# One instruction instead of two for the high and low parts of two neighbouring weight units

## The chip, the cores and the metric

The kernel runs on one core of a Trainium2 chip. The metric is the device time of one execution in microseconds (us); lower is better. Engines are named as in the profile: PE is TensorE (PEld its weight loads), DVE is VectorE, ACT is ScalarE, POOL is GpSimd, SP is SyncE, which here issues the weight transfers.

## The reference

Two transformer blocks run one after the other on 256 tokens of width 2048, in float32, and every dense product reads its weights once from HBM. Cut to its products:

```
# first block
h = rmsnorm(x);  qkv = h @ w_qkv                      # 2048 x 6144
y = [diff_attention, stick_breaking_attention, chunk_band_attention]
x = x + y @ w_o
h = rmsnorm(x)
g = causal_dwconv(h @ w_gate);  u = h @ w_up          # 2048 x 5632 each
x = x + (silu(g) * u) @ w_down
x = rmsnorm(x)
# second block
h @ w_in;  mla_mixer;  dsa_mixer (top-k keys);  x = x + [a, b] @ w_out
x = x + memory_cross_attention(rmsnorm(x), rmsnorm(mem))
x = x + square(relu(rmsnorm(x) @ w_up)) @ w_down      # d_ff = 8192
out = rmsnorm(x)
```

## The kernel before

**Units.** All weights are cut into 804 units. A unit is 128 rows by 1024 columns of float32 (512 KB; the eight units of the stage `tail` have 800 columns, the four of `k_nope` 512). Units form groups, one per pair of PSUM banks (`group_banks`): a "turned" group (`qk`, `gate`, `up1`, `up2` and others) has 4 units and writes a transposed result, a "straight" group (`v`, the `o`, `out` and `down` stages) has 2 to 8. All groups with more than one unit start at an even unit and end at an odd one.

**A unit's way.** PE multiplies in float32 with split operands: `w = hi + lo`. For each unit
- SP issues the transfer into one of 4 slots of `raw_w` (line 1705), once DVE has finished with the unit four before (semaphore `w_lo`, line 1704);
- ACT writes `hi_w` by a copy with rounding (`split_hi`, line 771). It first waits for the transfer, and for PE to have used the unit four before, whose slot it overwrites (`w_used`, line 770; PE raises it twice per unit, once per half);
- DVE writes `lo_w = raw_w - hi_w` (`split_lo`, line 1177) after `w_hi`;
- PE waits for `w_lo` (line 416) and does 16 matmuls (turned, lines 428 and 430) or 12 (straight, lines 437 to 439).

**Order.** There is no scheduler: each engine's program is written out by hand and is executed strictly in that order. `units(n)` stands in the programs of PE, ACT and DVE at corresponding places. On PE it runs the next n units. On ACT and DVE, for each unit u of them, it first splits unit u + 3 and then, if u is the last of its group, does the group's work: `turned_group` or `straight_group`. The split of u + 3 needs PE to be through with unit u - 1. Between the calls of `units` stand the attention steps, norms (`token_scales`, `pieces`, `root`), rotations and so on.

**Group work named below.** For `gate`, ACT and DVE alternate: ACT copies one half out of PSUM (L794), DVE adds the other (L1191), ACT scales for the convolution (L800), DVE adds two taps (L1196, L1199), all this for both halves; then ACT's tanh (L804) and DVE's product (L1204). `up1` and `up2` are shorter (L794, L1191, L1210 or L1215, then ACT L810 or L816 and DVE L1183). `down1_2` adds into the residual (L1235, L1238) and ACT takes sums of squares (L779), from which the next norm is made. In a step of the band attention PE does scores (L566), values (L612), a transposition (L596) and one unit; DVE does `soft` (L1433 to L1438) and `total` (L1457, on which the transposition of the same head waits), and then its share of `units(1)`.

## Time and profile before

| | |
|---|---|
| device time, median of 3 runs | 2481.21 us (2480.41 to 2484.02) |
| profiled execution: its time, its span | 2483.1 us, 2481.3 us |
| PE busy | 2417.3 us, 97% |
| DVE busy, ACT busy | 1500.9 us (60%), 1261.0 us (51%) |
| chain that ended last: PE, DVE, ACT | 94%, 2%, 2% of the span |
| mean granted TensorE clock | 0.992 of full speed |
| weight transfers | 424.7 MB, the 16 DMA engines 54.7% busy |

The span is what the profiler saw between the first and the last instruction. Because matmuls overlap, a busy PE is not PE at its peak; but idle time of PE in the waits is time in which nothing ran on it. An engine's row in the timeline gives start, duration, engine, line, operation and tiles, and in brackets how long the engine had been idle and who released it.

### The profile page before, as it was taken

To read this page: it belongs to the slowest core of one execution; us is meant where nothing else is said; L and a number is where in the kernel's file an instruction comes from. 1 tells how busy PE (TensorE), PEld (TensorE's weight loads), DVE (VectorE), ACT (ScalarE), POOL (GpSimd) and SP (SyncE) were. 2 spreads that over 40 slices of the span, in tenths; PEclk is the share of its full clock that TensorE was granted. 3 is DMA by queue.
4 is the path that set the end of the run, shared out by engine and by line. 5 is a ranking of instruction groups with operands and counts; after the bars stand their busy time and mean duration, and the time that the engine had idled before them with its cause. 6 is when DMAs were issued, how large, how long until landed. Compare 5 with 4: busy or idle time off the path is not lost.

```text
span 2481.3 us, 31755 instructions
## 1 busy us (share of the span) xinstructions
PE 2417.3 (97%) x12304; PEld 2020.1 (81%) x12304; DVE 1500.9 (60%) x2311; ACT 1261.0 (51%) x1974; POOL 5.2 (0%) x12
## 2 busy tenths in 40 slices
PE   6999999999999999999999999999999999999998
PEld 5888887788888888888877877787788888888886
DVE  5586777666666556645667544564666556556454
ACT  5466566655555435534556445555544444344343
POOL 0000000000000000000000000000000000000000
PEclk9999999999999999999999999999999999999999
DMA  6544444455555665565454544554566666666664
GB/s 211 174 162 158 136 154 147 150 188 177 197 180 191 189 189 187 192 205 185 155 180 144 178 128 134 173 169 136 160 179 193 189 187 184 194 185 191 206 187 141
DMA packets 118341, 432.11 MB, mean 174 GB/s; under 512 B 13184, under 2 KB 13328, under 8 KB 117680
## 3 DMA queue, kind: packets, MB, share of 16 engines
q1 hardware_dynamic: 117216, 424.70, 54.7%
q0 software_dynamic: 976, 5.39, 0.6%
q8 instruction: 98, 1.61, 0.3%
q14 instruction: 51, 0.42, 0.1%
HBM read 427.93 MB, written 2.11 MB: 173 GB/s over the span
## 4 chain that ended last, share of the span: by engine, by line
PE 94%; DVE 2%; ACT 2%; issue 1%; DMA 1%; ACTq 0%; SPq 0%; DVEq 0%
PE bank L428 29%; PE bank L437 15%; PE bank L439 15%; PE bank L438 15%; PE bank L430 15%; PE bank L612 1%; PE bank L454 1%; DVE lo_w L1177 1%; ACT hi_w L771 0%; PE bank L596 0%; PE bank L485 0%; DVE xT L1300 0%; PE bank L566 0%; PE bank L575 0%; PE bank L523 0%
## 5 line engine op out<-in xcount | busy, mean ns | idle before, releaser
L1177 DVE TENSOR_TENSOR lo_w<-raw_w,hi_w 128x1024 fp32r<-128x1024 f32 x804 | 968.1, 1219 | 689.8 <-ACT hi_w L771 689.0
L771 ACT ACTIVATE hi_w<-raw_w 128x1024 fp32r<-128x1024 f32 x804 | 834.0, 1053 | 678.7 <-PE bank L439 429.7
L428 PE MATMUL bank<-xT,hi_w 128*128 128x512 f32 x3008 | 1062.6, 398 | 2.9 <-DVE lo_w L1177 1.8
L430 PE MATMUL bank<-xT,lo_w 128*128 128x256 f32 x3008 | 843.6, 280 | 0.0
L428 PEld LDWEIGHTS bank<-xT,hi_w 128*128 128x128 f32 x3008 | 566.3, 188 | 139.0 <-issue 2.1
L430 PEld LDWEIGHTS bank<-xT,lo_w 128*128 128x128 f32 x3008 | 569.3, 189 | 0.2
L439 PE MATMUL bank<-hi_w,act_lo 128*128 128x512 f32 x864 | 341.2, 395 | 0.0
L438 PE MATMUL bank<-lo_w,act_hi 128*128 128x512 f32 x864 | 341.2, 395 | 0.0
L437 PE MATMUL bank<-hi_w,act_hi 128*128 128x512 f32 x864 | 341.2, 395 | 0.0
L437 PE MATMUL bank<-hi_w,xT 128*128 128x512 f32 (+1 forms) x736 | 295.0, 401 | 4.2 <-DVE xT L1300 3.4
L439 PE MATMUL bank<-hi_w,xT 128*128 128x512 f32 (+1 forms) x736 | 287.6, 391 | 0.0
L438 PE MATMUL bank<-lo_w,xT 128*128 128x512 f32 (+1 forms) x736 | 287.1, 390 | 0.0
L439 PEld LDWEIGHTS bank<-hi_w,act_lo 128*128 128x128 f32 x864 | 162.1, 188 | 39.5
L437 PEld LDWEIGHTS bank<-hi_w,act_hi 128*128 128x128 f32 x864 | 162.1, 188 | 39.4
L438 PEld LDWEIGHTS bank<-lo_w,act_hi 128*128 128x128 f32 x864 | 162.1, 188 | 39.4
L437 PEld LDWEIGHTS bank<-hi_w,xT 128*128 128x128 f32 x736 | 139.8, 190 | 32.1 <-issue 4.7
L439 PEld LDWEIGHTS bank<-hi_w,xT 128*128 128x128 f32 x736 | 139.3, 189 | 29.0
L438 PEld LDWEIGHTS bank<-lo_w,xT 128*128 128x128 f32 x736 | 139.7, 190 | 25.6
L1183 DVE TENSOR_TENSOR act_lo<-steps,act_hi 128x512 fp32r<-128x512 f32 x54 | 37.4, 692 | 39.3 <-ACT act_hi L816 23.3
L1300 DVE SCALAR_TENSOR_TENSOR xT<-bank,gains,xT 128x256 fp32r<-128x256 f32 x96 | 39.7, 476 | 20.8 <-ACT xT L872 20.6
L1230 DVE TENSOR_TENSOR x<-bank,x 128x512 f32<-128x512 f32 x80 | 51.2, 682 | 0.0
L794 ACT ACTIVATE product<-bank 128x256 f32<-128x256 f32 x88 | 33.4, 380 | 35.0 <-PE bank L430 35.0
(299 smaller groups left out, 1486.6 us busy)
## 6 DMA issues: line engine op xcount, KB each, us to landing
raw_w<-in_w_up SPq DMA_DIRECT2D x216, 512.0 KB, 4.2
raw_w<-in_w_down SPq DMA_DIRECT2D x216, 512.0 KB, 4.2
raw_w<-in_w_gate SPq DMA_DIRECT2D x88, 512.0 KB, 3.6
raw_w<-in_w_in SPq DMA_DIRECT2D x72, 512.0 KB, 3.8
raw_w<-in_w_qk SPq DMA_DIRECT2D x64, 512.0 KB, 3.6
raw_w<-in_w_v SPq DMA_DIRECT2D x32, 512.0 KB, 3.7
raw_w<-in_w_o SPq DMA_DIRECT2D x32, 512.0 KB, 3.6
raw_w<-in_w_out SPq DMA_DIRECT2D x32, 512.0 KB, 3.6
```

The lines of the kernel that those rows point to most:

```text
L428: e.matmul(pair[c][:, :], w_hi[:, cols_k], both[:, kt].rearrange("p h t -> p (h t)"), start=(kt == 0), stop=False, skip_group_check=True)
L430: last = e.matmul(pair[c][:, 0:TOK], w_lo[:, cols_k], both[:, kt, 0, :], start=False, stop=(kt == g.kts - 1), skip_group_check=True)
L437: e.matmul(out, in_hi[:, at, rows], w_hi[:, cols_k], start=(kt == 0), stop=False)
L438: e.matmul(out, in_hi[:, at, rows], w_lo[:, cols_k], start=False, stop=False)
L439: last = e.matmul(out, in_lo[:, at, rows], w_hi[:, cols_k], start=False, stop=(kt == g.kts - 1))
L454: last = e.transpose(bank[:, k * TOK + t * P:k * TOK + (t + 1) * P], src[:, t, kt * P:(kt + 1) * P], const("ident"))
L771: e.activation(hi_w[:, u % SPLIT_SLOTS, 0:unit_cols[u]], raw_w[:, u % RAW_SLOTS, 0:unit_cols[u]], ACT.Copy).then_inc(s["w_hi"], 1)
L794: e.activation(out, group_banks(n)[c][:, TOK:2 * TOK], ACT.Copy, scale=scale).then_inc(s["part_out"], 1)
L1177: e.tensor_tensor(lo, raw_w[:, u % RAW_SLOTS, 0:unit_cols[u]], hi.bitcast(F32), ALU.subtract).then_inc(s["w_lo"], 1)
L1183: e.tensor_tensor(lo, prod[:, pair % 2], hi.bitcast(F32), ALU.subtract).then_inc(s[f"act_lo{tag}_done"], 1)
L1230: e.tensor_tensor(here, bank[:, :], here, ALU.add).then_inc(s["x_added"], 1)
L1300: e.scalar_tensor_tensor(dst[:, dst0 + kt, 1, :], banks[4 + p % 4][:, k * TOK:(k + 1) * TOK], scale, dst[:, dst0 + kt, 0, :].bitcast(F32), ...
```

## The change

For two neighbouring units, an even one and the odd one behind it, ACT now writes both high parts with one instruction over the two slots (2048 columns), and DVE both low parts with one. `split_hi` and `split_lo` do nothing for an odd unit. `w_hi` and `w_lo` count pairs. Before it splits the pair (u, u + 1), ACT waits for both transfers, and for PE to have used both units whose slots are overwritten (`u - SPLIT_SLOTS + 2`). SP, which still issues one transfer per unit, waits for the pair in whose slots it loads. PE waits for `w_lo` only at even units. The slots stay four for each of the three buffers.

```diff
@@ tensor_program, units
-                    e.wait_ge(s["w_lo"], u + 1)
+                    if u % 2 == 0:
+                        e.wait_ge(s["w_lo"], u // 2 + 1)
@@ scalar_program
             def split_hi(u):
-                if u < n_units:
-                    e.wait_ge(s[f"raw_landed{u % RAW_SLOTS}"], 16 * (u // RAW_SLOTS + 1))
+                if u % 2 == 0 and u < n_units:
+                    a, cols = u % SPLIT_SLOTS, unit_cols[u]
+                    for n in (u, u + 1):
+                        e.wait_ge(s[f"raw_landed{n % RAW_SLOTS}"], 16 * (n // RAW_SLOTS + 1))
                     if u >= SPLIT_SLOTS:
-                        e.wait_ge(s["w_used"], 2 * (u - SPLIT_SLOTS + 1))
-                    e.activation(hi_w[:, u % SPLIT_SLOTS, 0:unit_cols[u]], raw_w[:, u % RAW_SLOTS, 0:unit_cols[u]],
-                                 ACT.Copy).then_inc(s["w_hi"], 1)
+                        e.wait_ge(s["w_used"], 2 * (u - SPLIT_SLOTS + 2))
+                    e.activation(hi_w[:, a:a + 2, 0:cols], raw_w[:, a:a + 2, 0:cols], ACT.Copy).then_inc(s["w_hi"], 1)
@@ vector_program
             def split_lo(u):
-                if u < n_units:
-                    hi, lo = (w[:, u % SPLIT_SLOTS, 0:unit_cols[u]] for w in (hi_w, lo_w))
-                    e.wait_ge(s["w_hi"], u + 1)
-                    e.tensor_tensor(lo, raw_w[:, u % RAW_SLOTS, 0:unit_cols[u]], hi.bitcast(F32),
+                if u % 2 == 0 and u < n_units:
+                    a, cols = u % SPLIT_SLOTS, unit_cols[u]
+                    hi, lo = (w[:, a:a + 2, 0:cols] for w in (hi_w, lo_w))
+                    e.wait_ge(s["w_hi"], u // 2 + 1)
+                    e.tensor_tensor(lo, raw_w[:, a:a + 2, 0:cols], hi.bitcast(F32),
                                     ALU.subtract).then_inc(s["w_lo"], 1)
@@ sync_program
-                    e.wait_ge(s["w_lo"], u - RAW_SLOTS + 1)
+                    e.wait_ge(s["w_lo"], (u - RAW_SLOTS) // 2 + 1)
```

ACT's order before, in the stages `gate` and `up1` (one `up1` group, then one `gate` group; `product` and `steps` are buffers of the group work, `hi_w` the split):

```order
L771 ACTIVATE hi_w<-raw_w 128x1024 [waits w_used,raw_landed2]
L794 ACTIVATE product<-bank 128x256 [waits conv_taps,w_used] x2
L810 ACTIVATE act_hi<-steps 128x512 [waits prod1]
L771 ACTIVATE hi_w<-raw_w 128x1024 [waits w_used,raw_landed3]
L771 ACTIVATE hi_w<-raw_w 128x1024 [waits w_used,raw_landed0]
L771 ACTIVATE hi_w<-raw_w 128x1024 [waits w_used,raw_landed1]
L771 ACTIVATE hi_w<-raw_w 128x1024 [waits w_used,raw_landed2]
L794 ACTIVATE product<-bank 128x256 [waits prod1,w_used]
L800 ACTIVATE steps<-product,gains 128x256 [waits sum_out]
L794 ACTIVATE product<-bank 128x256 [waits prod1,w_used]
L800 ACTIVATE steps<-product,gains 128x256 [waits sum_out]
L804 ACTIVATE steps<-steps 128x512 [waits conv_taps]
```

The same place after the change (lines are moved by three):

```order
L775 ACTIVATE hi_w<-raw_w 128x2048 [waits w_used,raw_landed3,raw_landed2]
L797 ACTIVATE product<-bank 128x256 [waits conv_taps,w_used] x2
L813 ACTIVATE act_hi<-steps 128x512 [waits prod1]
L775 ACTIVATE hi_w<-raw_w 128x2048 [waits w_used,raw_landed1,raw_landed0]
L775 ACTIVATE hi_w<-raw_w 128x2048 [waits w_used,raw_landed3,raw_landed2]
L797 ACTIVATE product<-bank 128x256 [waits prod1,w_used]
L803 ACTIVATE steps<-product,gains 128x256 [waits sum_out]
L797 ACTIVATE product<-bank 128x256 [waits prod1,w_used]
L803 ACTIVATE steps<-product,gains 128x256 [waits sum_out]
L807 ACTIVATE steps<-steps 128x512 [waits conv_taps]
```

Four splits between two groups' work have become two of double width; the one that stands right ahead of a group's work is now a pair, and waits for the last unit of that group instead of the last but one.

DVE's order before at the same place:

```order
L1204 SCALAR_TENSOR_TENSOR steps<-steps 128x512 [waits gate_tanh]
L1177 TENSOR_TENSOR lo_w<-raw_w,hi_w 128x1024 [waits w_hi] x4
L1191 SCALAR_TENSOR_TENSOR product<-bank,product 128x256 [waits part_out] x2
L1210 SCALAR_TENSOR_TENSOR steps<-steps,product 128x512 [waits sum_out,gate_silu]
L1183 TENSOR_TENSOR act_lo<-steps,act_hi 128x512 [waits act_hi1_done]
```

And after:

```order
L1209 SCALAR_TENSOR_TENSOR steps<-steps 128x512 [waits gate_tanh]
L1182 TENSOR_TENSOR lo_w<-raw_w,hi_w 128x2048 [waits w_hi] x2
L1196 SCALAR_TENSOR_TENSOR product<-bank,product 128x256 [waits part_out] x2
L1215 SCALAR_TENSOR_TENSOR steps<-steps,product 128x512 [waits sum_out,gate_silu]
L1188 TENSOR_TENSOR act_lo<-steps,act_hi 128x512 [waits act_hi1_done]
```

DVE keeps its order in the same way: nothing but the splits is merged, and the second of the two pairs stands right ahead of the group's first addition.

## Rows read from the trace of the kernel before

**Rows 1.** Page, part 1: busy us, share of the span, instructions.

```profile
PE 2417.3 (97%) x12304; PEld 2020.1 (81%) x12304; DVE 1500.9 (60%) x2311; ACT 1261.0 (51%) x1974; POOL 5.2 (0%) x12
```

**Rows 2.** Waits of PE: total us, times, longest us.

```profile
PE bank L454 <- ACT y L862: 14.3, 1, 14.3
PE bank L454 <- DVE h_nat L1290: 7.9, 2, 3.9
...
PE bank L428 <- DVE lo_w L1177: 1.8, 1, 1.8
```

**Rows 3.** Groups by form: busy us, mean ns, idle before with releaser.

```profile
L1177 DVE TENSOR_TENSOR lo_w<-raw_w,hi_w 128x1024 fp32r<-128x1024 f32 x792 | 957.4, 1224 | 683.6 <-ACT hi_w L771 682.9
...
L771 ACT ACTIVATE hi_w<-raw_w 128x1024 fp32r<-128x1024 f32 x792 | 824.5, 1056 | 671.6 <-PE bank L439 422.6 <-PE bank L430 246.3 <-DMA raw_w<-in_w_out 2.4
...
L1183 DVE TENSOR_TENSOR act_lo<-steps,act_hi 128x512 fp32r<-128x512 f32 x54 | 37.4, 692 | 39.3 <-ACT act_hi L816 23.3 <-ACT act_hi L810 16.0
...
L804 ACT ACTIVATE steps<-steps 128x512 f32<-128x512 f32 x22 | 13.9, 633 | 22.5 <-DVE steps L1199 22.5
```

**Rows 4.** Timeline of ACT at a gate group's end.

```profile
788.63 1.06 ACT L771 ACTIVATE hi_w<-raw_w 128x1024 fp32r<-128x1024 f32 x1 [1.51 <-PE bank L430]
791.46 1.06 ACT L771 ACTIVATE hi_w<-raw_w 128x1024 fp32r<-128x1024 f32 x1 [1.77 <-PE bank L430]
...
797.83 0.63 ACT L804 ACTIVATE steps<-steps 128x512 f32<-128x512 f32 x1 [1.07 <-DVE steps L1199]
798.37 2.94 ACT L771 ACTIVATE hi_w<-raw_w 128x1024 fp32r<-128x1024 f32 x3
```

**Rows 5.** Timeline of DVE there.

```profile
793.70 0.42 DVE L1191 SCALAR_TENSOR_TENSOR product<-bank,product 128x256 f32<-128x256 f32 x1
...
799.45 3.50 DVE L1177 TENSOR_TENSOR lo_w<-raw_w,hi_w 128x1024 fp32r<-128x1024 f32 x3 [0.26 <-ACT hi_w L771]
```

**Rows 6.** Timeline of ACT in two straight stages, v and down1_2.

```profile
82.12 1.06 ACT L771 ACTIVATE hi_w<-raw_w 128x1024 fp32r<-128x1024 f32 x1 [1.66 <-PE bank L439]
84.84 1.06 ACT L771 ACTIVATE hi_w<-raw_w 128x1024 fp32r<-128x1024 f32 x1 [1.66 <-PE bank L439]
...
1182.53 1.06 ACT L771 ACTIVATE hi_w<-raw_w 128x1024 fp32r<-128x1024 f32 x1 [1.74 <-PE bank L439]
1185.33 1.06 ACT L771 ACTIVATE hi_w<-raw_w 128x1024 fp32r<-128x1024 f32 x1 [1.74 <-PE bank L439]
```

**Rows 7.** Timeline of PE: after a wait for lo_w, and at the mix norm.

```profile
19.40 0.50 PE L428 MATMUL bank<-xT,hi_w 128*128 128x512 f32 x1 [1.82 <-DVE lo_w L1177]
...
1213.08 3.22 PE L454 MATMUL bank<-consts,mixed 128*128 128x128 f32 x14 [5.44 <-DVE mixed L1290]
```

**Rows 8.** Timeline of DVE at the last down1_2 group.

```profile
1206.74 0.68 DVE L1235 TENSOR_TENSOR h_nat<-bank,x 128x512 f32<-128x512 f32 x1
```

**Rows 9.** Windows: PE busy, PEld, DVE, ACT, POOL, then PEclk, DMA share, GB/s.

```profile
21.00:22.00 1.00, 1.00 (x5) 0.86 (x4) 1.00 (x4) 1.00 (x4) 0.00 (x0) 0.50 0.91 348
1609.00:1610.00 1.00, 0.00 (x0) 0.00 (x0) 1.00 (x2) 0.55 (x1) 0.00 (x0) 1.00 0.00 0
1612.00:1613.00 1.00, 1.00 (x3) 0.79 (x3) 1.00 (x2) 1.00 (x2) 0.00 (x0) 0.50 0.78 123
```

**Rows 10.** Timelines of the band attention, PE then DVE.

```profile
382.78 0.39 PE L596 MATMUL bank<-consts,a_p 128*128 128x128 f32 x2
...
382.83 0.42 DVE L1433 CUSTOM_DVE_ANT_0 a_s<-bank,rel 128x256 f32<-128x256 f32 x1
383.69 0.48 DVE L1438 SCALAR_TENSOR_TENSOR a_s<-a_s,a_small,a_p 128x256 f32<-128x256 f32 x1
384.48 0.29 DVE L1457 CUSTOM_DVE_ANT_0 a_p<-a_p,a_s 128x128 f32<-128x128 f32 x1 [0.31 <-ACT a_s L908]
```

**Rows 11.** Page, part 6: issues, KB each, median us to landing.

```profile
raw_w<-in_w_up SPq DMA_DIRECT2D x216, 512.0 KB, 4.2
mem<-in_mem POOLq DMA_DIRECT2D x1, 2048.0 KB, 9.1
```

## Prediction

> **What bounds the kernel.** I read the page's busy times first: PE 97%, DVE 60%, ACT 51% [rows 1]. Then the waits of PE: the reader is to see that what PE waits for are norms (L454 with L862 and L1290), and that in 804 units it waited for a low part once, 1.8 us at the start [rows 2]. The splits cost PE nothing. The groups by form say why: before the 792 wide splits on ACT the engine had been idle 671.6 us in all, and what ended that was PE giving a slot free; DVE was idle 683.6 us, ended by ACT [rows 3]. So the splits run as early as the slots allow, and the question is how early that still is after the change. For this I read the timelines around one gate group.
>
> **PE's pace.** ACT's splits start when PE has finished a unit, so their distance is PE's time per unit: 788.63 to 791.46, 2.83 us turned [rows 4]; 2.72 and 2.80 us straight [rows 6].
>
> **What the change removes.** Neither engine limits, so only latency counts, but the instructions first. A high part takes 1.056 us for 1024 columns, and 512 columns 0.633: 0.83 ns a column, so 2048 take 1.056 + 0.85 = 1.91 us. A low part takes 1.224 and 0.692 us: 2.29 us for 2048 [rows 3]. Single splits back to back have a distance of 0.94 us on ACT ((2.94 - 1.06) / 2) and 1.14 on DVE ((3.50 - 1.22) / 2) [rows 4, 5], so that two take 2.00 and 2.36. A pair saves 0.09 and 0.07 us; over 402 pairs 36 and 28 us of engines which are idle 40 and 49%. I cost it at nothing for PE.
>
> **What it adds: the lead.** Call T the time at which PE ends an odd unit u. Before, at that time units u+1 and u+2 were ready, and u+3, whose slot was free since T - 2.83, mostly too; a split had 3 units of PE's time minus its own 2.3 us, some 6 us to spare. Now ACT may begin the pair (u+3, u+4) only at T, and it ends at T + 0.07 + 1.91 = T+1.98. DVE runs T+2.02 to T+4.31. PE has (u+1, u+2) to do, to T+5.66 (turned), T+5.44 or T+5.6 (straight). Spare: 1.3, 1.1, 1.3 us. Where ACT and DVE have nothing else to do, that is enough, in `up2` and `down` too: `up2` has ACT at work until about T+6.5 (L816), which puts the next low part at about T+10.8, and PE wants it at T+11.3. But what stands in ACT's queue ahead of a pair now counts after 1.1 to 1.3 us instead of 6.
>
> **Term 1, gate, 22 groups.** Before, from DVE's first addition (793.70) to the end of tanh (797.83 + 0.63 = 798.46) the group's work takes 4.76 us, ACT and DVE handing each other every step [rows 4, 5]. That chain starts behind the low part that stands ahead of it; now this is a pair that ends at T+4.31. So: addition T+4.23 (instructions overlap by 0.08), tanh ends T+8.99, and only then does ACT reach the pair (u+5, u+6), whose slots were free at T+5.66: high part T+8.90 to T+10.81, low part to T+13.14. PE is through with (u+3, u+4) at T+11.3 and waits 1.85 us. To refill PE takes about 0.3 more: neighbouring units otherwise overlap by some 0.2 us (an estimate), and the first matmul after such a wait took 0.50 us [rows 7] instead of 0.40. 2.14 us. The following up1 group's chain is through by about T+18.6, before the next pair may start (T+18.9), so nothing adds up and nothing is caught up: PE was never ahead of anything. 22 x 2.14 = **47 us**.
>
> **Term 2, the clock after such waits.** The trace of before shows what an idle PE does to the granted clock. After the 1.82 us wait before 19.40 the clock was 0.50, that is 1.2 instead of 2.4 GHz, in the window 21 to 22; while PE stood still at 1609 to 1610 it was 1.00, and at 1612 to 1613, with PE busy again, 0.50 [rows 7, 9]. Windows around these show about 3.2 us at the lower level each time, beginning after PE was back: 1.6 us lost. Gate's waits are close to the shortest of these. Bounds: 0 to 22 x 1.6 = 35 us. I take six in ten, **21 us**.
>
> **Term 3, norms.** At the ends of `o_late`, `down1_2` and `ox` nothing hides the chain to the next norm. Before, the last DVE addition group began at 1206.74 and PE's transpositions at 1213.08, 6.34 us later [rows 7, 8]; PE had ended its unit at about 1207.6, so T is about 1208. Now DVE must first do the pair, whose slots are free only at T: the addition starts at T+4.2 (T+3.3 for the 800-column units) and not at T-1.3. About 4.4 us each, **13 us**. In the bursts behind `o_late` and `ox` the last quarter of the transposed input stands behind a pair again: PE finishes transposing and one unit at T+3.7, DVE's part is done at T+5.9; 2 x 2.5 = **5 us**.
>
> **Term 4, band attention.** In an odd step DVE ends the pair at T+4.31; then soft of the next head (wide, 382.83 to 384.17, 1.2 us without its wait) and total (0.29) end at about T+5.7. PE's transposition, which needs total, would be due at T+4.75 (steps of 3.9 us; it stood 0.9 us behind the unit's end, at 382.78 [rows 10]). 0.95 us, in 8 steps; in the three of these where an `o_early` group ends, DVE's two additions (1.28 us) stand between. **12 us**.
>
> **Term 5, the other places.** About 30 pairs in other attention steps (diff, stick-breaking, dsa, the index scores, the start of cross), in the rotation of the index key, in the squares of `down1_2` and in the prologue have a chain through ACT and DVE behind them that PE waits on within about one unit. Bounds: 0 each where other waits cover it, and DVE's whole 2.3 us. I take band's value, the nearest, rounded up for the groups that end there: 30 x 1.1 = **33 us** (0 to 69).
>
> The sum is 47 + 21 + 13 + 5 + 12 + 33 = 131 us on the profiled execution's own 2483.1 us (span 2481.3), which is 1.9 us above the median of 2481.21: **2612 us** against the median.
>
> The Trainium skill ("Perfetto Trace Analysis", Optimizing Scalar/DVE Operations) says both things on this change: grouping into larger operations helps where the engine is saturated, and where ACT and DVE are not saturated but cause bubbles on other engines, breaking instructions up may let work finish sooner. The trace puts this kernel in the second case (60 and 51% busy). By the first sentence alone the result would be no slower; by the second it is slower, as summed.
>
> **Rivals.**
> - *The lead is enough.* 4.31 us is less than 5.44, and the group work might slip in elsewhere. For: in `up2` and `down`, half of the units, the arithmetic says so. Against: gate's chain is read from rows and is longer than the spare. Then nothing changes: 2481 us.
> - *Faster.* PE's 64 us of idle time (2481.3 - 2417.3) end mostly with an ACT or DVE chain. If in the dense attention steps it is the number of instructions that sets the pace, the 0.16 us saved per pair lie on the path: at most some 70 attention pairs x 0.16 = 11 us, 2470 us. The point from which this decides is PE waiting in these steps before; it waited next to nothing there [rows 2].
> - *Only gate and norms.* The attention steps absorb the rest, and the clock holds: 2481 + 47 + 13 = 2541 us.
> - *The clock falls every time and attention is at its bound*: 35 instead of 21, 69 instead of 33, some 10 more for the clock after the longer waits: 2481 + 131 + 14 + 36 + 10 = 2672 us.
> - *Transfers.* Two are now issued at once, when a pair's low part is done, and must have landed 6.6 to 7 us later. One takes 4.2 us [rows 11]. If two take twice that, 8.4, a pair needs 8.4 + 4.3 = 12.7 us per two periods of 10.9 to 11.3: over 200 x 1.6, 2800 us and more. Against: 2048 KB took 9.1 us [rows 11], so that a further 512 KB costs (9.1 - 4.2) / 3 = 1.6 us and a pair some 5.8.
> - *Not done as said*: that the wide form is slower than its columns. ACT and DVE rows at 512 and 1024 lie on a line; each 0.3 us more on a pair takes 22 x 0.3 = 7 us.
>
> The Trainium skill ("VectorE: DVE Perf Modes", the TRN2 errata) has one large tile pay a fixed cost once and many small ones each time, and gives (N + 151) / 0.96 ns for a float32 tensor_tensor. This trace agrees: 1224 ns for 1024; for 2048 the formula gives 2.29 us, an estimate of that page. As a reason to merge it is worth the 0.07 us above, off PE's path.
>
> **Numbers.** Slower as summed, with its own range 2560 to 2665: 0.68. Only gate and norms: 0.14. All at their bounds: 0.07. Transfers: 0.03. The lead is enough: 0.05. Faster: 0.03. A measurement of this kernel tells 0.2%, 5 us, from no change. Slower by more than that 0.92, within it 0.05, faster 0.03. The range 2535 to 2668 leaves out the transfers, the last two and half of the tails.
>
> **What will show it.** Right: PE's waits on DVE's low part appear some 22 times with about 1.8 us each in the gate and up1 stage, in which a pair of groups takes about 2.1 to 3.7 us longer, and none in `up2` and `down`; the splits' mean is 1.9 and 2.3 us; PE busy time is nearly unchanged except for the lower clock; norm waits have grown by 4 us. Wrong: waits for lo_w also in `up2` or `down` (my 1.3 us is no spare), transfers that release ACT's splits, or no waits at gate. The weakest part is term 5.

## The result, and the profile after

| | before | after |
|---|---|---|
| median (lowest to highest), 4 runs each | 2481.49 us (2480.41 to 2484.02) | 2675.73 us (2673.27 to 2677.62) |
| ratio, 95% interval | | 1.0782 (1.0769 to 1.0796) |
| span of the profiled execution | 2481.3 us | 2673.6 us |
| PE busy; PE idle (span less busy) | 2417.3; 64.0 us | 2472.7; 200.9 us |
| mean granted TensorE clock | 0.992 | 0.968 |

The change makes the kernel 194 us slower. The forecast was 2612 us with a range up to 2668: the direction was right, the size was 64 us short, and the result lies 8 us beyond the range.

The page's busy times of the changed kernel answer to [rows 1]:

```profile
PE 2472.7 (92%) x12304; PEld 2052.9 (77%) x12304; DVE 1443.5 (54%) x1909; ACT 1183.0 (44%) x1572; POOL 5.2 (0%) x12
```

ACT and DVE work less than before, 78 and 57 us less in all. PE has the same 12304 matmuls, is busy 55.4 us longer with them, and idle 137 us longer. These two sum to the 192 us of the spans. Its waits (total us, times, longest us) answer to [rows 2]:

```profile
PE bank L429 <- DVE lo_w L1182: 44.1, 22, 3.5
PE bank L455 <- DVE h_nat L1295: 18.7, 2, 9.4
PE bank L455 <- ACT y L865: 14.3, 1, 14.3
PE bank L597 <- DVE a_small L1462: 12.2, 8, 2.7
PE bank L455 <- DVE mixed L1295: 9.8, 1, 9.8
PE bank L438 <- DVE xT L1305: 8.6, 3, 3.8
...
PE bank L438 <- DVE lo_w L1182: 6.5, 5, 1.9
```

Before, there were two waits for a low part, 1.8 us at the start and another one of 0.7 us at 1247.11, which the prediction overlooked. Now there are 27. 22 of them stand behind the gates: 1.3 to 2.3 us each, 44.1 us together. (The first row has 22 waits and 44.1 us as well, but only by chance: it holds 20 of the gates' waits, 3.5 us at the start of the program and one of 0.3; the other two gates are in the last row, with three waits of 0.9 us in `down1_2`.) Beside them stands a long list of waits for other things, nearly all of them ended by ACT or DVE. The norms' waits have grown from 7.9 to 18.7 and from 5.4 to 9.8 (the second is the mix norm of [rows 7]). The first y wait, 14.3 us, is what it was.

The groups by form (busy us, mean ns, idle before with its releasers) answer to [rows 3]:

```profile
L1182 DVE TENSOR_TENSOR lo_w<-raw_w,hi_w 128x2048 fp32r<-128x2048 f32 x396 | 907.2, 2292 | 996.8 <-ACT hi_w L775 996.0
...
L775 ACT ACTIVATE hi_w<-raw_w 128x2048 fp32r<-128x2048 f32 x396 | 757.2, 1912 | 929.6 <-PE bank L440 554.3 <-PE bank L431 363.2 <-DMA raw_w<-in_w_up 4.6
```

The wide forms cost what their columns predict, 1.91 and 2.29 us. ACT's idle time before them is ended by PE giving slots free. A transfer ended 4.6 us of it by this row, which names the three largest releasers, and 12.1 of 945.5 us by ACT's complete list of waits.

**One gate group.** The timelines of ACT, DVE and PE of the changed kernel there answer to [rows 4, 5], with T at 869:

```profile
869.02 1.92 ACT L775 ACTIVATE hi_w<-raw_w 128x2048 fp32r<-128x2048 f32 x1 [3.63 <-PE bank L431]
...
877.31 0.64 ACT L807 ACTIVATE steps<-steps 128x512 f32<-128x512 f32 x1 [1.07 <-DVE steps L1204]
877.85 1.90 ACT L775 ACTIVATE hi_w<-raw_w 128x2048 fp32r<-128x2048 f32 x1
```

```profile
870.97 2.29 DVE L1182 TENSOR_TENSOR lo_w<-raw_w,hi_w 128x2048 fp32r<-128x2048 f32 x1 [3.25 <-ACT hi_w L775]
873.18 0.42 DVE L1196 SCALAR_TENSOR_TENSOR product<-bank,product 128x256 f32<-128x256 f32 x1
...
879.78 4.57 DVE L1182 TENSOR_TENSOR lo_w<-raw_w,hi_w 128x2048 fp32r<-128x2048 f32 x2 [1.11 <-ACT hi_w L775]
```

```profile
882.13 0.50 PE L429 MATMUL bank<-xT,hi_w 128*128 128x512 f32 x1 [2.13 <-DVE lo_w L1182]
```

The gate's chain begins at T+4.2 and ends at T+9.0, ACT reaches the next pair only then (877.85, with nothing idle before it), DVE ends its low part at T+13.1, and PE has stood for 2.1 us. This is the working of the first term to within 0.1 us, except for the wait itself (2.0 on average against 1.85).

**The clock.** Windows of 1 us around the next gate's wait of 1.93 us, which ended at 906.93 (PE busy, PEld, DVE, ACT, POOL, then the granted clock, DMA share, GB/s), answer to [rows 9]:

```profile
906.00:907.00 1.00, 0.07 (x1) 0.07 (x1) 0.88 (x1) 1.00 (x2) 0.00 (x0) 1.00 0.00 0
907.00:908.00 1.00, 1.00 (x6) 0.87 (x7) 0.94 (x1) 0.58 (x3) 0.00 (x0) 1.00 0.36 33
...
909.00:910.00 1.00, 1.00 (x5) 0.90 (x4) 1.00 (x3) 0.00 (x0) 0.00 (x0) 0.50 0.94 377
910.00:911.00 1.00, 1.00 (x5) 0.81 (x4) 0.71 (x2) 0.15 (x1) 0.00 (x0) 0.50 1.04 422
...
912.00:913.00 1.00, 1.00 (x7) 0.88 (x6) 0.20 (x1) 0.00 (x0) 0.00 (x0) 1.00 1.00 352
```

PE comes back at the full clock, and from 909 to 911 has 0.50, 1.2 instead of 2.4 GHz. With the windows to the left and right of these two, 1.7 us of the full clock are lost. The same followed 11 of the 22 gates' waits, by windows of 1 us over the whole stage.

**Where it stands still in attention.** The timelines of ACT, DVE and PE of the changed kernel in the band attention answer to [rows 10], with T at 404.3:

```profile
404.34 1.91 ACT L775 ACTIVATE hi_w<-raw_w 128x2048 fp32r<-128x2048 f32 x1 [1.76 <-PE bank L440]
```

```profile
403.08 0.16 DVE L1465 RECIPROCAL a_small<-a_small 128x1 f32<-128x1 f32 x1
406.28 2.29 DVE L1182 TENSOR_TENSOR lo_w<-raw_w,hi_w 128x2048 fp32r<-128x2048 f32 x1 [3.04 <-ACT hi_w L775]
408.49 0.42 DVE L1438 CUSTOM_DVE_ANT_0 a_s<-bank,rel 128x256 f32<-128x256 f32 x1
```

```profile
404.15 0.70 PE L567 MATMUL bank<-qkT 64*128 64x256 f32 x2
410.09 0.33 PE L597 MATMUL bank<-consts,a_p 128*128 128x128 f32 x1 [0.89 <-DVE a_small L1462]
```

DVE is done at 403.24, and the next head's softmax (L1438) stands behind the pair's low part in its program. The pair waits for ACT, ACT waits for PE to end the pair's *second* unit, and so DVE stands 3.04 us before it works 2.29 us on the pair. The softmax's scores are there at 404.85, and it runs at 408.49, 3.6 us later; before, the scores were there at 382.58 (`L566`) and the softmax ran at 382.83 [rows 10]. So the merged pair, with its wait, is a piece of queue that the attention's own instructions stand behind. Term 4 of the prediction has this case, with the transposition (L597) at T+5.7; it came at T+5.8. How much ACT stands there before the ffn burst, by its waits: first before, then after.

```profile
ACT hi_w L771 <- PE bank L439: 27.0, 22, 2.8
ACT hi_w L771 <- PE bank L430: 26.4, 21, 2.4
```

```profile
ACT hi_w L775 <- PE bank L431: 85.3, 26, 5.8
ACT hi_w L775 <- PE bank L440: 81.0, 28, 10.8
```

53.4 us in 43 waits have become 166.3 us in 54.

### The profile page after: what moved, and what is told of

Same layout as the page of the kernel before. It is cut to its first block, busy times and chain, and to the rows that moved or that the text cites. A ratio compares the mean times of both kernels' runs of the same rounds, so it can differ in the third digit from the quotient of the medians.

```text
span 2673.6 us, 30498 instructions
## 1 busy us (share of the span) xinstructions
PE 2472.7 (92%) x12304; PEld 2052.9 (77%) x12304; DVE 1443.5 (54%) x1909; ACT 1183.0 (44%) x1572; POOL 5.2 (0%) x12
## 4 chain that ended last, share of the span: by engine, by line
PE 73%; DVE 12%; ACT 9%; issue 5%; DMA 1%; ACTq 0%; DVEq 0%; POOL 0%; SPq 0%
PE bank L429 21%; PE bank L438 13%; PE bank L440 13%; PE bank L439 13%; PE bank L431 10%; ACT hi_w L775 6%; DVE lo_w L1182 6%; ACT steps L803 1%; PE bank L455 1%; DVE steps L1201 1%; DVE steps L1204 1%; PE bank L613 1%; DVE x L1235 1%; DVE product L1196 1%; DVE xT L1305 0%
## 5 line engine op out<-in xcount | busy, mean ns | idle before, releaser
L1182 DVE TENSOR_TENSOR lo_w<-raw_w,hi_w 128x2048 fp32r<-128x2048 f32 (+1 forms) x402 | 917.0, 2282 | 1013.3 <-ACT hi_w L775 1012.5
L775 ACT ACTIVATE hi_w<-raw_w 128x2048 fp32r<-128x2048 f32 (+1 forms) x402 | 765.5, 1904 | 945.5 <-PE bank L440 567.7
L429 PE MATMUL bank<-xT,hi_w 128*128 128x512 f32 x3008 | 1082.4, 404 | 49.2 <-DVE lo_w L1182 44.1
L429 PEld LDWEIGHTS bank<-xT,hi_w 128*128 128x128 f32 x3008 | 576.7, 192 | 193.6 <-DVE lo_w L1182 51.1
L431 PEld LDWEIGHTS bank<-xT,lo_w 128*128 128x128 f32 x3008 | 579.2, 193 | 0.2
L438 PE MATMUL bank<-hi_w,xT 128*128 128x512 f32 (+1 forms) x736 | 301.5, 410 | 9.9 <-DVE xT L1305 8.6
L440 PE MATMUL bank<-hi_w,xT 128*128 128x512 f32 (+1 forms) x736 | 292.3, 397 | 0.0
L438 PEld LDWEIGHTS bank<-hi_w,xT 128*128 128x128 f32 x736 | 143.7, 195 | 40.7 <-issue 9.2
L440 PEld LDWEIGHTS bank<-hi_w,xT 128*128 128x128 f32 x736 | 142.1, 193 | 30.3
L819 ACT ACTIVATE act_hi<-steps 128x512 fp32r<-128x512 f32 x32 | 20.2, 632 | 103.7 <-DVE steps L1220 103.7
L803 ACT ACTIVATE steps<-product,gains 128x256 f32<-128x256 f32 x44 | 26.5, 602 | 78.4 <-DVE product L1196 78.4
```

Of the source, the lines that this page charges most:

```text
L429: e.matmul(pair[c][:, :], w_hi[:, cols_k], both[:, kt].rearrange("p h t -> p (h t)"), start=(kt == 0), stop=False, skip_group_check=True)
L431: last = e.matmul(pair[c][:, 0:TOK], w_lo[:, cols_k], both[:, kt, 0, :], start=False, stop=(kt == g.kts - 1), skip_group_check=True)
L438: e.matmul(out, in_hi[:, at, rows], w_hi[:, cols_k], start=(kt == 0), stop=False)
L440: last = e.matmul(out, in_lo[:, at, rows], w_hi[:, cols_k], start=False, stop=(kt == g.kts - 1))
L775: e.activation(hi_w[:, a:a + 2, 0:cols], raw_w[:, a:a + 2, 0:cols], ACT.Copy).then_inc(s["w_hi"], 1)
L803: e.activation(conv1[:, pair % 2, c], out, ACT.Identity, bias=gain("convb", tile), scale=gain("conv2", tile)).then_inc(s["conv_base"], 1)
```

## The experiments

Unless said otherwise, they start from the changed kernel, written so that the form of a pair is chosen by its number p, on each engine: `wide` is the change's form; `one` is two instructions, each at its own place with its own wait, as before; `twin` is two instructions of 1024 columns at the pair's place. `w_hi` and `w_lo` count units again, and a wide instruction adds 2, which changes no wait.

All results in one table. The columns behind the ratio are stage lengths of each profile: up to the ffn burst; ffn burst, gate, up1, down1 ("ffn"); mix norm to dsa and out ("mix"); memory and cross attention ("mem"); ox; mlp burst, up2, down2, end ("mlp"). They end where PE's transpositions of the next norm begin.

| kernel | us | ratio to before (95%) | start | ffn | mix | mem | ox | mlp |
|---|---|---|---|---|---|---|---|---|
| before | 2481.5 | 1 | 460.6 | 752.5 | 397.0 | 108.1 | 28.3 | 734.8 |
| after | 2675.7 | 1.0782 (1.0769-1.0796) | 515.0 | 830.8 | 431.7 | 125.7 | 35.0 | 735.4 |
| 1 single, pair's waits | 2710.7 | 1.0922 (1.0905-1.0938) | 524.6 | 845.2 | 434.9 | 126.3 | 38.0 | 742.4 |
| 2 wide in ffn only | 2567.1 | 1.0346 (1.0331-1.0362) | 465.7 | 834.5 | 397.4 | 108.1 | 28.3 | 734.9 |
| 3 wide from unit 548 | 2491.7 | 1.0042 (1.0027-1.0058) | 461.1 | 753.3 | 396.1 | 106.6 | 33.7 | 737.0 |
| 4 single at 22 pairs | 2625.9 | 1.0586 (1.0568-1.0603) | 515.5 | 775.4 | 432.2 | 126.6 | 35.3 | 735.6 |
| 5 third slot pair in ffn | 2619.9 | 1.0562 (1.0539-1.0585) | 516.3 | 769.7 | 434.2 | 126.9 | 35.2 | 737.3 |
| 6 wide on ACT only | 2613.6 | 1.0532 (1.0512-1.0553) | 484.6 | 819.4 | 422.5 | 119.5 | 31.9 | 734.8 |
| 7 wide on DVE only | 2601.6 | 1.0483 (1.0465-1.0502) | 489.6 | 794.7 | 418.2 | 123.4 | 36.2 | 735.5 |
| 8 waits filled | 2675.4 | 1.0781 (1.0759-1.0804) | 515.3 | 820.5 | 435.6 | 125.9 | 35.2 | 740.5 |
| 9 only the place | 2516.1 | 1.0145 (1.0127-1.0162) | 476.3 | 749.4 | 407.6 | 115.9 | 31.1 | 730.6 |
| 10 one step later | 2605.2 | 1.0500 (1.0485-1.0514) | 475.2 | 832.6 | 415.1 | 106.9 | 34.5 | 739.0 |
| 11 wide from unit 560 | 2484.7 | 1.0014 (1.0005-1.0023) | 460.8 | 752.4 | 396.9 | 108.1 | 28.3 | 736.4 |
| 12 before, third slot pair | 2482.4 | 1.0007 (0.9997-1.0016) | 459.3 | 753.2 | 396.3 | 106.6 | 29.9 | 733.1 |
| 13 = 5 and 10 | 2538.3 | 1.0228 (1.0214-1.0242) | 476.6 | 766.2 | 416.5 | 106.5 | 34.4 | 736.5 |
| 14 before, one step later | 2491.1 | 1.0037 (1.0025-1.0050) | 464.5 | 752.2 | 404.5 | 106.5 | 29.0 | 733.7 |
| 15 = 2 with filled waits | 2551.6 | 1.0279 (1.0265-1.0293) | 465.6 | 815.7 | 397.0 | 108.1 | 28.3 | 734.9 |

### 1. Single instructions with the pair's waits

```
 def hi_form(p), lo_form(p):
-    return 'wide'
+    return 'twin'    # waits of the pair, then two instructions of 1024 columns
```

> The split of a pair is again two instructions of 1024 columns on each engine, as before the change, but with the waits of the changed kernel: both units' weights landed and both units' slots used before the first of them starts, VectorE starts when both high parts are there, and TensorE when both low parts are. If the lost lead is the cause (a slot pair is given back only when its second unit is used), the time is that of the changed kernel or a little over it, since a pair takes 2 x 1.06 + 2 x 1.22 = 4.6 us in place of 4.3: 2670 to 2720 us, and TensorE waits for low parts again. If the wide instruction itself is the cause (its form, or what two engines do at the same time over 2048 columns), the time goes back to 2481 to 2500 us.

2710.7 us. The loss is all there, and 35 us more, without a single wide instruction. So it is the waits, and not the form: that the wide form is slower than its columns, or disturbs something, is out. The wide form by itself is the better one, as its 0.16 us a pair says.

### 2 and 3. Wide in one stretch of the program

```
-    return 'wide'
+    return 'wide' if 128 <= p < 392 else 'one'     # 2
+    return 'wide' if p >= 548 else 'one'           # 3
```

> Wide pairs only in the units of gate, up1 and down1 (128 to 391); everywhere else one instruction for each unit, as before. If the stages' differences between the two traces are each the stage's own, this gives 2481 + 78 = 2559 us (2550 to 2570). If only the 22 waits after the gates count (the prediction's first term), 2481 + 44 to 47 = 2525 to 2530 us. If the slower clock is one effect of the whole program rather than of each wait, the time lies elsewhere, above 2570.

> Wide pairs only in up2 and down2 (units 548 to 803, a third of all), one instruction for each unit elsewhere. Lost lead: these stages have a spare of 1.1 to 1.3 us left and show no wait, so 2481 to 2484 us, no change. Were the wide form or the paired transfers the cause, a third of the loss of 194 us would show: 2530 to 2545 us.

2567.1 and 2491.7 us. In 2 the ffn stage has the changed kernel's length (834.5 against 830.8) and every other stage after it the old one: the loss is local to each stage. 3 was expected at no change and came out 9 us slower than the kernel before in the same session (2482.3). The table has 5.4 of them in ox, before the mlp norm. PE's timeline of kernel 3 there:

```profile
1750.84 1.51 PE L466 MATMUL bank<-consts,h_nat 128*128 128x128 f32 x6 [9.40 <-DVE h_nat L1314]
```

9.40 us in place of 3.9: the pairs around this burst do what the third term says of a norm. That I had put the start of the wide stretch in front of the norm was my oversight; number 11 moves it.

### 4. Single instructions at 22 pairs

```
+    return 'one' if p % 8 == 0 and (136 <= p <= 256 or 296 <= p <= 336) else 'wide'
```

These are the pairs behind a gate's chain.

> The changed kernel, with the 22 pairs whose split stands behind a gate's chain on both engines (the third pair after each gate group) split by one instruction for each unit. If the chain that holds back the pair's low part is the wait of 1.9 to 2.1 us after each gate, these waits go to 0 to 0.5 us: 2676 - 22 x 2 = 2632 us if the clock stays as low in this stage, and 2676 - 60 to 78 = 2598 to 2616 us if the low clock there comes from these waits. If another thing (transfers, the form) makes them: 2665 to 2680 us.

2625.9 us, 50 less with 22 of 402 pairs changed, and between the two times that I had given for a clock that stays low and one that recovers. What is left of the waits for low parts at the pairs made single (L1201; ten waits, nine of them 0.3 to 0.4 us and one 0.95):

```profile
PE bank L440 <- DVE lo_w L1201: 3.4, 9, 1.0
...
PE bank L449 <- DVE lo_w L1201: 0.3, 1, 0.3
```

The stage is 55.4 us shorter. PE's busy time in it went from 771.4 to 754.9, 16.5 us less, and its idle time by 38.9. By windows of 1 us the clock no longer falls behind a gate, so I put the 16.5 us down to it. The gates' part of the loss is measured by this.

### 5. A third pair of slots

```
+RINGS = ((140, 352),)      # in these units hi_w and lo_w have 6 slots; the two more lie in h_nat1's memory
-                        e.wait_ge(s["w_used"], 2 * (u - SPLIT_SLOTS + 2))
+                        e.wait_ge(s["w_used"], 2 * (before_of[u] + 2))   # the unit before in the same slot
```

The two programs split a pair two units earlier there; `raw_w` keeps four slots, and the loads come in pairs.

> The changed kernel with wide pairs everywhere, and in units 140 to 351 a third pair of slots for the high and low parts (memory that is free there), so that a pair's split starts one pair of units earlier (5.4 us). Lost lead: the 20 waits behind the gates in that stretch go to 0 and with them the low clock: 2676 - 20 x (2.0 + 0.75) = 2621 us (2612 to 2632), although every instruction of the split is as wide as before. If the wide form makes the waits: 2665 to 2680 us. If the loads are late, since the raw weights still have four slots, TensorE waits for low parts at other places and it lies between.

2619.9 us. Every split is as wide as in the changed kernel, the loads come in pairs as there, and 21 of the 22 waits behind the gates are gone; the one left, 2.3 us at 551, lies ahead of the third slot pair. With number 1 this closes the square for these waits: single instructions with the pair's lead have them, wide ones with more lead don't. It also rules out the wide form and the pairing of the loads as their cause. The stage is still 17 us longer than before: that first gate, one new wait of 2.4 us in its burst, three in `down1_2` (3.5), 4.4 more at the mix norm, and 4 us of PE's busy time. The Trainium skill ("Perfetto Trace Analysis", Optimization Strategy) says that the same gap repeating on the engine which should be saturated can mean that memory for the next tile is short, buffer count included. Here that holds: 22 gaps of about 2 us, and one more pair of slots removed 21 of them.

### 6 and 7. Wide on one engine only

```
 hi_form: 'wide'   lo_form: 'one'     # 6
 hi_form: 'twin'   lo_form: 'wide'    # 7, each of ACT's two with the wait for its own slot
```

> ScalarE makes the high parts of a pair with one instruction (it starts when both slots are free, T, where T is the end of the pair's second unit on TensorE); VectorE makes the low parts one unit at a time, the second one a step later in its program. Lost lead: the first low part is there at T + 1.98 + 1.22 = T + 3.2, so 2.3 us are left where the changed kernel has 1.1 to 1.3; after a gate the chain holds the second low part until about T + 9.2 and TensorE wants it at T + 8.2, a wait of 1 us, 22 times. Time about 2481 + 22 + some 40 in the other stages: 2540 us (2515 to 2590). If the loss is all VectorE's wide instruction: 2481 to 2490; if all ScalarE's: 2665 to 2680.

> The reverse: ScalarE makes the two high parts with two instructions that stand behind each other in its program, each with the wait for its own slot alone, so that the first runs before T and the second at T; VectorE makes both low parts with one instruction at T + 1.1 to T + 3.4. Lost lead: spare 2.1 us in place of 1.1 to 1.3; behind a gate's chain both high parts (2.1 us) and the low parts (2.3) still stand behind each other and the pair is there at T + 12.6 where it is wanted at T + 11.3, a wait of 1.3 us, 22 times. Time about 2481 + 29 + some 60 in the other stages: 2570 us (2530 to 2620). If the loss is all ScalarE's wide instruction: 2481 to 2490; if all VectorE's: 2665 to 2680.

2613.6 and 2601.6 us, the first 24 us above the range that I gave, the second inside its range. Each engine's half costs over 60% of the whole, so the halves don't add: either is enough to tie the second unit's end to the first one's split. In 6 I had put 1 us on each gate. PE there waits for low parts of turned units 45.7 us in 29 waits, 1.4 to 2.1 us at a gate; the second unit's low part stands in DVE's program behind the whole gate chain.

### 8 and 15. The waits filled with matmuls

```
+                    if u % 8 == 0 and (136 <= u <= 248 or 296 <= u <= 328):
+                        ...            # wait for the bank, as the group's first matmul does
+                        for _ in range(4):
+                            e.matmul(pair[0][:, :], xT[:, 0, 0, 0:P], xT[:, 0].rearrange("p h t -> p (h t)"),
+                                     start=True, stop=False, skip_group_check=True)
```

> The changed kernel, and at 20 of the 22 waits behind a gate TensorE does four extra matmuls of 512 columns (their result is overwritten, 4 x 0.4 = 1.6 us) ahead of the wait for the low part, so that it stands idle 0.4 to 0.5 us there in place of 2.0. Nothing else changes, and the low part comes at the same time. If the lower clock after a wait is brought on by the idle time of that wait, it stays at 1.00 there and the time falls by 20 x 0.75 = 15 us (0.75 us a wait is what the run with the 22 pairs split singly showed in TensorE's busy time): 2655 to 2665 us. If the clock has another cause: 2674 to 2680 us. If the extra matmuls run into the wait's end, more than 2680.

2675.4 us: no change. PE's timeline of kernel 8 at one gate, then windows of its clock behind the next gate, and behind the one after that, which has no filling:

```profile
872.57 1.11 PE L429 MATMUL bank<-xT 128*128 128x512 f32 x4
...
874.81 0.50 PE L446 MATMUL bank<-xT,hi_w 128*128 128x512 f32 x1 [1.12 <-DVE lo_w L1203]
```

```profile
901.00:902.00 1.00, 1.00 (x8) 0.86 (x7) 1.00 (x1) 0.00 (x0) 0.00 (x0) 1.00 0.75 225
...
926.00:927.00 1.00, 1.00 (x4) 0.78 (x3) 1.00 (x2) 0.00 (x0) 0.00 (x0) 0.50 0.83 299
```

The four matmuls overlap and take 1.1 us, not 1.6, so 1.1 us of idle time is left; they end before the low part comes, as meant. The clock stays at 1.00 behind all 20 filled waits; of the two without filling (2.1 and 2.3 us, ended at 924.69 and 1164.67) the first is followed by 0.50. The distance from gate to gate, which in the changed kernel alternated between some 24.7 and 26.3 us (waits that end at 855.95, 882.13, 906.93 and 933.25), is 24.7 to 25.3 now. The stage is 10.3 us shorter, but in this profile mix and mlp are 3.9 and 5.1 longer. Why is not known: in `up2` the matmuls of 512 columns take 399 ns on average against 394 in the changed kernel, at a granted clock of 1.00 in both, but the kernel before has 399 there too, in an mlp stage of 734.8 us. To separate this, number 15 does the same in kernel 2, where the rest of the program is as before:

> Wide pairs in units 128 to 391 alone, with TensorE's four extra matmuls ahead of 20 of the 22 waits; without them this kernel took 2567 us. If the idle time of the wait brings the low clock, and the low clock costs the 10 us that the profile of the filled run showed in this stage: 2554 to 2560 us. If the gain is given back elsewhere: 2565 to 2570.

2551.6 us, 15.5 under number 2 by the medians (19 by the profiles), with all other stages equal to 0.4 us, and a little under the range that I gave. Again no filled wait is followed by the low clock, and one of the two unfilled ones is. So the clock's share is real: it is brought on by the idle time of these waits, and costs 15 to 19 us in this stage, with the 16.5 of number 4 between.

### 9. Only the place in the program

```
 'twin' on both engines, each of the two instructions waits for its own unit alone, and so does PE:
+                for k in range(n):
+                    e.wait_ge(s["w_used"], 2 * (u + k - SPLIT_SLOTS + 1))
+                    e.activation(hi_w[:, a + k, 0:cols], raw_w[:, r + k, 0:cols], ACT.Copy).then_inc(s["w_hi"], 1)
```

> Only the order of the changed kernel: both units of a pair are split at the same place of ScalarE's and VectorE's programs (one step early for the second), but by one instruction for each unit, each with the waits for its own unit alone, and TensorE waits for each unit. The first unit of a pair is then as early as before the change. Behind the gates: second low part at T + 2.3, chain until T + 7.1, next pair at T + 9.4, wanted at T + 11.3: no wait, so the stage of gate, up1 and down1 stays at 752.5 us. If the loss in the attention stages (54 us before the ffn burst, 35 in the mix stages) comes from the order, in which the two engines stand at a slot's wait while attention's own instructions are queued behind it: 2560 to 2600 us. If it comes from the time at which the parts are there: 2481 to 2500 us.

2516.1 us, between the two ranges. No low part is late but the first of the program, and the ffn stage has no loss, as worked out. In attention and mix the place alone, with single instructions that are early for the first unit, costs 15.7 of 54.4 and 10.6 of 34.7 us. Before the ffn burst ACT stands, in its waits for a slot:

```profile
ACT hi_w L787 <- PE bank L440: 70.2, 50, 4.0
ACT hi_w L787 <- PE bank L449: 57.4, 44, 6.5
```

127.6 us, against 53.4 before and 166.3 in the changed kernel, for 15.7 us of loss in place of 54.4. So the time that ACT stands isn't itself the cost: most of the loss comes only together with the late and long pair behind it. The Trainium skill ("Perfetto Trace Analysis", Optimizing Scalar/DVE Operations) says that breaking up instructions may let work finish sooner, where ACT and DVE are not saturated but cause bubbles elsewhere. This run agrees: 2516 against 2676 us, from broken-up instructions at the same places. Number 1 shows the condition: broken up, but with the pair's waits kept, they take 2711 us.

### 10. The wide split one step later

```
+def late(p): return 4 <= p < 128 or 392 <= p < 548
-                    split_hi(u + SPLIT_SLOTS - 1)
+                    for v in (u + 2, u + 3):
+                        if v % 2 == 0 and late(v) == (v == u + 2):
+                            split_hi(v)                              # and split_lo likewise
```

> The changed kernel, with the wide split one unit's step later in both programs, in the attention and mix units alone (4 to 127 and 392 to 547): the slots' wait is nearly over when the engines come to it, and what belongs to attention runs first. If the loss in those stages comes from the order (engines standing at the wait), about half of the 54 + 35 + 18 + 7 us of them goes: 2610 to 2640 us. If it comes from the lost lead, the parts are later still and it grows: 2680 to 2730 us.

2605.2 us: 70 us gained by moving each wide split *later*. ACT's standing before the ffn burst is now

```profile
ACT hi_w L791 <- PE bank L455: 17.8, 9, 3.5
...
ACT hi_w L791 <- PE bank L446: 13.7, 4, 3.6
```

and the stage is 14.6 us over the kernel before instead of 54.4. Of these, 4.7 are at the norm (8.7 us in place of 3.9), 7.7 in waits for low parts (9.6 us in six in place of 1.8), and 2.6 in PE's busy time. In these stages the place of the pair's wait in the queue cost more than a step of lead is worth; the result is 5 us below the range that I gave.

### 11 and 12. Is there anything to win?

```
+    return 'wide' if p >= 560 else 'one'     # 11
+    'one' everywhere, RINGS = ((140, 352),)  # 12: the kernel before with the third slot pair
```

> Wide pairs only from unit 560 on, past the burst of the mlp norm; the run with wide pairs from 548 on was 9 us over the kernel before, 5.4 of it in that norm's wait (9.4 us in place of 3.9) and 1.4 in a wait for a low part. If these pairs alone made it: 2480 to 2484 us, the time of the kernel before, though 122 pairs (three in ten) are wide. If the wide form or the loads in pairs cost something everywhere: 2487 to 2492.

> The kernel before the change with the third pair of slots in units 140 to 351, one instruction for each unit. In that stage TensorE of the kernel before waits for almost nothing (746.8 of 752.5 us busy, clock 1.00), so more lead has nothing to give: 2479 to 2484 us. Anything under 2476 would mean that the lead was short before the change too.

2484.7 us (ratio 1.0005 to 1.0023) and 2482.4 us (0.9997 to 1.0016). 122 wide pairs in `up2` and `down2` cost next to nothing: 3 us, just above my range, of which 0.7 us are seen in three waits of 0.24 for a low part. So 6 of the 9 us of number 3 were the pairs at the norm. More lead than before gives nothing in the ffn stage, where 12 has it.

### 13. Both remedies

> Both remedies at once, every pair still split by wide instructions: the split one step later in the attention and mix units, and the third slot pair in units 140 to 351. If the two causes are independent, the gains add: 2676 - 70 - 56 = 2550 us (2543 to 2557). If one hides the other (the slower clock, say, or a common wait), less: 2570 to 2605.

2538.3 us, 137 under the changed kernel with every split still wide. The gains of 10 and 5 are 70.5 and 55.8, together 126: neither takes from the other, and 11 us come on top, more than I had forecast. By the stages 5 of them lie in ffn and 4 in mlp, which neither remedy touches and where profiles of unchanged code differ by as much.

### 14. Before, with its single splits one step later

> The kernel before the change with its single splits one step later in the attention and mix units (4 to 127, 392 to 547). ScalarE of the kernel before stands 53 us in these waits before the ffn burst. If standing there costs time before the change too: 2470 to 2478 us. If the lead is then what is short (each split starts a step later): 2490 to 2520. If neither: 2481.

2491.1 us, 10 slower, so less standing is no gain there. With single splits the lead is what is short if the place moves later (PE now waits 14.6 us for low parts, 2.5 before). The place chosen there was the better one; no version found beats it.

## Why the prediction was short

**Right.** *The lead.* T, the spare of 1.1 to 1.3 us, and that nothing else changes: numbers 1 and 5. *Term 1*, 47 forecast, 44 measured: 22 waits of about 2 us behind the gates, by the chain that I named. The timeline has it step by step, and numbers 4 and 5 remove it. *Term 2 for the gates*, 21: 16.5 in number 4 and 15.5 in number 15. The forecast of 1.6 us six times in ten was near: the low clock followed 11 of the 22 waits, and made that distance 1.6 us longer. *Term 3*, 13 and 5: the three norms' waits grew by 15.2 (7.9 + 5.4 became 18.7 + 9.8), and the bursts behind `o_late` and `ox` have a new wait of 2.3 us each for transposed input, 4.0 net. *Term 4*, 12: the eight waits of the band's transposition sum to 12.2. *`up2` and `down`*: 735.4 against 734.8, and number 11. Transfers and the wide form's own cost stayed out, as said.

**Wrong, step 1: term 5, "30 x 1.1 = 33 us".** PE's idle time grew by 137 us. Take off the gates' 44, the norms' 15, the bursts' 4 and the band's 12, and 61 are left for "the other places", 28 more than I took, if below the bound of 69. I had given each of them the band's price. In the band it was right, but most of the others aren't like the band. PE's waits of both kernels, one by one, show where the 61 us lie: 20 before the ffn burst, 3 in ffn, 25 in mix, 13 in mem. They are some 43 new or longer waits in place of 30, and ten of them grew by 2.3 to 5.4 us each, 34 us together. The three longest of these are transpositions around the memory attention, first before, then after:

```profile
PE bank L454 <- DVE h_x L1327: 2.5, 1, 2.5
PE bank L454 <- ACT bank L779: 2.4, 1, 2.4
PE bank L454 <- DVE h_x L1290: 0.6, 1, 0.6
```

```profile
PE bank L455 <- DVE h_x L1332: 7.0, 1, 7.0
PE bank L455 <- ACT bank L782: 6.4, 1, 6.4
PE bank L455 <- DVE h_x L1295: 6.0, 1, 6.0
```

5.5 us have become 19.4. What makes the last one are DVE's additions ahead of that norm, before and after, while PE starts its last unit ahead of it at 1633.3 and 1806.3:

```profile
1633.10 1.28 DVE L1230 TENSOR_TENSOR x<-bank,x 128x512 f32<-128x512 f32 x2
```

```profile
1808.51 2.29 DVE L1182 TENSOR_TENSOR lo_w<-raw_w,hi_w 128x2048 fp32r<-128x2048 f32 x1 [2.48 <-ACT hi_w L775]
1810.72 1.28 DVE L1235 TENSOR_TENSOR x<-bank,x 128x512 f32<-128x512 f32 x2
```

They came with the start of that unit and now come 4.4 us after it, behind the pair. This is term 3's chain at term 3's price, 4 to 5 us, at places that I had left in term 5 at 1.1 each. So the step that failed is the size: one price, from the place where the chain behind the pair is nearly hidden, for places where it isn't. Numbers 9 and 10 show that the place of the pair's wait in the program is part of it; number 10 takes off 70 us by that alone, and brings mem from 125.7 back to 106.9.

**Wrong, step 2: term 2, counted behind the gates only.** PE was busy 55.4 us longer with the same matmuls, and I forecast 21. Behind the gates it is 16.5; the other 39 follow the waits of norms, bursts and attention (16.6 us up to the ffn burst, 9.9 in mix, 5.1 in mem, and 8 in the rest of ffn, by the windows' busy times). The windows of before and after up to the ffn burst (PE busy, then clock, DMA share, GB/s):

```profile
0.00:460.60 460.60, 435.23 (x2272) 0.99 0.51 164
```

```profile
0.00:515.00 515.00, 451.80 (x2273) 0.96 0.42 147
```

I had found that even 1.8 us of idle time can be followed by the low level, and then applied it to one kind of wait. 28 and 34 us, less 1 or 2 by which the other terms together came out below their forecasts, are the 61 by which the sum of 131 was short of the spans' 192. The rival "at their bounds", 2672 us, had both of these and was the nearest; 0.07 was too little for it. The range ended just below the result for the same reason.

**Open.** Why kernel 8 gave its 10 us back in stages that it doesn't touch. Where the 11 us on top in number 13 come from. And the cause at each of term 5's places: the waits are measured one by one, but only whole stages were changed by a run, and the 39 us of busy time outside the gates' waits are put down to the clock by the granted clock of the stages, not by a run of their own.

## What to carry to other kernels

Merging the refills of two neighbouring buffers takes lead twice: the merged one starts when the *second* buffer is free, and until then what stands behind it in the programs of both engines waits with it. With four slots and three engines in strict order, 0.16 us saved on a pair of instructions cost the kernel 7.8%, so before merging, list what stands behind the wait in each queue, and add slots or move the wait later if anything does. And once a wait of 2 us appears on PE, price the clock behind it for every such wait, not for the regular ones alone: here it was 55 us on 137 us of idle time.

## What the runs showed of the hardware

- A lasting stop isn't needed for the low clock. Of 22 waits of 1.3 to 2.3 us, some 25 us apart with PE fully busy in between, 11 were followed by a few us at 0.50, the shortest of these 11 being 1.9 us long. Each cost 1.7 us of the full clock.
- With matmuls ahead of the same wait (1.1 to 1.5 us left idle) the level stayed at 1.00 behind all 20 filled waits in number 8 and all 20 in number 15, and fell behind one of the two unfilled waits in each. In number 7, whose 22 waits at the gates are 1.3 to 1.8 us long, it didn't fall behind any of them.
- At a granted clock of 1.00 the same matmul's mean still differed by 1% between profiles (394 ns in the changed kernel and 399 in the kernel before and in number 8, for 512 columns in `up2`).
- Four matmuls of 512 columns with 128 x 128 weights, issued back to back in number 8, take 1.1 us together, although each is shown with 0.40.
